# One gap below the large SBUF buffers: every large buffer at a multiple of 512 bytes

## The reference

```python
h = x
for i in range(2):
    if i == 0:
        h = h + retention_branch(rms_norm(h, ret_norm), ret_w_in, ret_w_out)
    else:
        h = h + pool_branch(rms_norm(h, pool_norm), pool_w_in, pool_w_group, pool_scale, pool_w_out)
    gate = sigmoid(rms_norm(h, ple_norm[i]) @ ple_w_gate[i])
    h = h + gate * (p[i] @ ple_w_proj[i])
return rms_norm(h, final_norm)
```

## Time and profile before

| | |
|---|---|
| time, median of 3 runs | 1616.88 us (1616.85 to 1617.04) |
| span of the profiled execution, first to last instruction | 1614.2 us |
| TensorE busy | 1592.1 us, 99% |
| TensorE weight loads busy | 1317.2 us, 82% |
| VectorE busy | 988.7 us, 61% |
| ScalarE busy | 726.6 us, 45% |
| granted TensorE clock, mean | 0.998 |
| from HBM | 296.60 MB, 185 GB/s over the span |

### The profile page before, as it was taken

How to read it: one execution, slowest core, us unless ns; L and a number is a source line. 1 busy time by engine, 2 the same in 40 slices (tenths; PEclk the granted TensorE clock), 3 DMA queues, 4 the chain that set the end, 5 groups by cost and what they waited for, 6 DMA issues and landing times.

```text
span 1614.2 us, 19583 instructions
## 1 busy us (share of the span) xinstructions
PE 1592.1 (99%) x7240; PEld 1317.2 (82%) x7240; DVE 988.7 (61%) x1218; ACT 726.6 (45%) x888; POOL 5.1 (0%) x13
## 2 busy tenths in 40 slices
PE   7999999999999999999999999999999999999997
PEld 6888888888888888888888888888888888888885
DVE  5676666657566666657656565645565565555665
ACT  6444434344444434345645444344434443445543
POOL 0000000000000000000000000000000000000000
PEclk9999999999999999999999999999999999999999
DMA  9545554545545455545455445555554555555451
GB/s 354 177 166 180 186 197 168 195 163 193 182 171 182 182 185 178 194 181 204 160 179 209 183 183 180 185 182 191 184 186 170 206 182 182 198 192 186 179 188 73
DMA packets 42806, 299.24 MB, mean 185 GB/s; under 512 B 4848, under 2 KB 4864, under 8 KB 7312
## 3 DMA queue, kind: packets, MB, share of 16 engines
q1 hardware_dynamic: 41408, 292.60, 50.5%
q0 software_dynamic: 1072, 5.06, 0.8%
q10 hardware_dynamic: 288, 1.05, 0.2%
HBM read 296.60 MB, written 2.10 MB: 185 GB/s over the span
## 4 chain that ended last, share of the span: by engine, by line
PE 98%; DVE 1%; DMA 1%; ACT 0%; issue 0%; SPq 0%; ACTq 0%
PE accB L303 11%; PE accB L304 11%; PE accB L305 11%; PE accC L303 10%; PE accC L304 10%; PE accC L305 10%; PE accA L303 10%; PE accA L305 10%; PE accA L304 10%; PE side L326 2%; DMA h<-in_x_dram 1%; PE side L368 0%; PE side L366 0%; PE side L367 0%; PE side L415 0%; PE side L416 0%
## 5 line engine op out<-in xcount | busy, mean ns | idle before, releaser
L799 DVE TENSOR_TENSOR w_lo<-w_raw,w_hi 128x1024 fp32r<-128x1024 f32 x552 | 669.7, 1223 | 424.4 <-ACT w_hi L566 420.0
L566 ACT CAST w_hi<-w_raw 128x1024 fp32r<-128x1024 f32 x552 | 579.3, 1054 | 628.0 <-PE accB L305 266.7
L303 PE MATMUL accA<-w_hi,xa_hi 128*128 128x512 f32 x512 | 201.2, 393 | 0.9 <-DVE w_lo L799 0.9
L305 PE MATMUL accA<-w_hi,xa_lo 128*128 128x512 f32 x512 | 199.7, 390 | 0.0
L304 PE MATMUL accA<-w_lo,xa_hi 128*128 128x512 f32 x512 | 199.7, 390 | 0.0
L303 PE MATMUL accC<-w_hi,xa_hi 128*128 128x512 f32 x384 | 150.7, 392 | 0.0
L304 PE MATMUL accC<-w_lo,xa_hi 128*128 128x512 f32 x384 | 149.6, 390 | 0.0
L305 PE MATMUL accC<-w_hi,xa_lo 128*128 128x512 f32 x384 | 149.5, 389 | 0.0
L304 PE MATMUL accB<-w_lo,xa_hi 128*128 128x512 f32 x384 | 149.4, 389 | 0.0
L303 PE MATMUL accB<-w_hi,xa_hi 128*128 128x512 f32 x384 | 149.4, 389 | 0.0
L305 PE MATMUL accB<-w_hi,xa_lo 128*128 128x512 f32 x384 | 149.4, 389 | 0.0
(11 more groups left out here) (183 smaller groups left out, 2120.3 us busy)
## 6 DMA issues: line engine op xcount, KB each, us to landing
w_raw<-in_stream_dram SPq DMA_DIRECT2D x275, 1024.0 KB, 4.8
h<-in_x_dram SPq DMA_DIRECT2D x4, 512.0 KB, 9.8
w_raw<-in_stream_dram SPq DMA_DIRECT2D x2, 512.0 KB, 7.2
dec<-in_decay_dram POOLq DMA_DIRECT2D x1, 1024.0 KB, 8.7
fgain<-in_final_gain_dram POOLq DMA_DIRECT2D x1, 1024.0 KB, 5.1
out_dram<-emb ACTq DMA_DIRECT2D x2, 512.0 KB, 3.1
out_dram<-emb SPq DMA_DIRECT2D x2, 512.0 KB, 2.6
bnd_raw<-in_band_dram POOLq DMA_DIRECT2D x1, 768.0 KB, 7.8
```

What stands on the lines that cost most here:

```text
L303: pe.matmul(acc[pair][t][:], xh, wh, start=first and b == 0, stop=False)
L305: mm = pe.matmul(acc[pair][t][:], xl, wh, start=False, stop=last and b == UNIT - 1)
L566: act.copy(w_hi[:, r % RING, :], w_raw[:, r // 2, (r % 2) * 1024:(r % 2 + 1) * 1024]).then_inc(hi_ready, 1)
L799: dve.tensor_tensor(w_lo[:, r % RING, :], w_raw[:, r // 2, (r % 2) * 1024:(r % 2 + 1) * 1024], w_hi[:, r % RING, :].bitcast(F32), ALU.subt ...
```

## The change

The small buffers, and `warm` from the end, are asked for first. Behind them comes one padding buffer of as many bytes as the next multiple of 512 wants, rounded down to 32-byte steps, since each buffer begins at a multiple of 32 anyway: here 32 bytes. `idn` is then at 16512 (remainder 128), `w_raw` at 19968 and the arena at 179712, both at remainder 0, and so is every other large buffer. No instruction is added, removed or moved.

```diff
+        idn = sb("idn", [P, P], F32)
+        gain = sb("gain", [P, STAGES - 1, KD], F32)
+        pscale = sb("pscale", [P, GROUPS * KG], F32)
...
+        junk = sb("junk", [P, TT, COL], mybir.dt.bfloat16)
+        warm = sb("warm", [P, 1], F32)
+        LINE = 512
+        sb("line_pad", [P, (-nc.sbuf_base % LINE) // 32 * 8], F32)
         w_raw = sb("w_raw", [P, RAW, PIECE * COL], F32)
         w_hi = sb("w_hi", [P, RING, UNIT * COL], F32R)
         w_lo = sb("w_lo", [P, RING, UNIT * COL], F32R)
...
         sig = sb("sig", [P, TT, COL], F32)
         p_raw = sig[:].rearrange("p t (k n) -> p t k n", n=SEQ)
-        idn = sb("idn", [P, P], F32)
...
-        junk = sb("junk", [P, TT, COL], mybir.dt.bfloat16)
-
-
         ARENA_KB = 48
         arena0 = nc.sbuf_base
+        assert arena0 % LINE == 0
         sb("arena", [P, ARENA_KB * 256], F32)
-        warm = sb("warm", [P, 1], F32)
```

More of the change, by code:

```diff
@@ L99, in sem @@
             return ctx.enter_context(nc.semaphore(name))
+        idn = sb("idn", [P, P], F32)
+        gain = sb("gain", [P, STAGES - 1, KD], F32)
+        pscale = sb("pscale", [P, GROUPS * KG], F32)
+        ssq = sb("ssq", [P, STAGES, TT, NC], F32)
+        rs = sb("rs", [P, STAGES, TT], F32)
+        stats = sb("stats", [P, TT, 6], F32)
+        mv = sb("mv", [P, TT, 2], F32)
+        rstd = sb("rstd", [P, TT], F32)
+        nx2 = sb("nx2", [P, TT], F32)
+        nt2 = sb("nt2", [P, TT], F32)
+        ni2 = sb("ni2", [P, TT], I32)
+        junk = sb("junk", [P, TT, COL], mybir.dt.bfloat16)
+        warm = sb("warm", [P, 1], F32)
+        LINE = 512
+        sb("line_pad", [P, (-nc.sbuf_base % LINE) // 32 * 8], F32)
         w_raw = sb("w_raw", [P, RAW, PIECE * COL], F32)
```

## The result

The changed kernel takes 1607.13 us (median of 4 runs, 1606.89 to 1607.45) against 1616.87 us for the kernel before on the same chip: a ratio of 0.9941, with a 95% interval of 0.9926 to 0.9955. It is faster by 9.7 us, the interval reaching from 7.3 to 12.0 us. The forecast was 1609.0.

What follows compares the result with a forecast made beforehand. TensorE's matmul count times start-to-start distance was taken as the bound. Arena matmuls 7.7 us plus transitions 0.2 us, all else zero, gave 7.9 us less: 1609.0 us from the 1616.88 median, 8-in-10 range 1602 to 1617.5.

Steps and rivals of the forecast that it cites:

- equal remainders: Main case: matching stationary and streamed remainders in the arena gives 1609.0 us, own range 1607.5 to 1610.5; 65%.
- What bounds the kernel: TensorE, busy 1592.1 of 1614.2 us: time is the number of matmuls times their start-to-start distance.
- Which remainder counts: Whether the remainder against the other operand or against 512 sets the matmul distance; the prediction chose the other operand.
- The arena's matmuls, 7.7 us: 1152 matmuls with `xb` and `dT` go from 233.35 to 226.67 ns each, gaining 7.7 us.
- Transitions, net 0.2 us gained: Disturbances at 0.04 us each: 13 fewer at arena returns and `values`, 9 more behind transposes in `xb` and `dT` stages.
- Transposes, nothing: `idn` stays at 128 while its partners move to 0; no effect, though 6.7 ns on all 320 would be 2 us.
- The other 5472 stationary operands, zero: `xa`, `oT`, `pT` matmuls keep equal remainders, so no change; bounds 73 us down and 37 us up.
- VectorE, ScalarE, transfers: No address effect on both engines; weight landings hidden; only x at the start exposed, +-0.3 us.
- Nothing moves: Rival: the arena's 6.7 ns comes from something else, such as its high place in memory; 1616.9 us, 11%.
- Zero is better than merely equal: Rival: operands off a multiple of 256 or 512 cost extra; 1520.9 us at full price, near 1565 at half; 14%.
- Slower: Rival: at remainders 0 and 0 the stream doesn't settle at 226.7 ns, costing 5472 matmuls 24 to 37 us; 1633 to 1646; 10%.

Runs made afterwards that it cites:

- the kernel at 448: Changed kernel with padding chosen so all large buffers and the arena begin 448 bytes past a multiple of 512; 1608.26 us, ratio 0.9949.
- the kernel with 192 bytes of padding: Kernel before, old buffer order, with only 192 bytes of padding between junk and the arena, putting the arena at remainder 128; 1608.51 us, ratio 0.9954.
- the last experiment: Changed kernel with pscale asked for ahead of idn, so idn too is at a multiple of 256; 1608.78 us, ratio 0.9952.
- the kernel at 128: Changed kernel with padding chosen so all large buffers and the arena begin 128 bytes past a multiple of 512; 1608.36 us, ratio 0.9948.

## Why the prediction was right, and where a term was off

The forecast gain was 7.9 us and the measured one 9.7. The time of 1607.1 us lies in the range for 8 in 10, but just outside the 1607.5 to 1610.5 us that the prediction gave equal remainders by themselves. Between the spans the gain is 8.6 us: the transitions brought 1.0 us more than forecast, the steady distance 0.1 less, the start and the rest 0.2 less. The other 1.1 us is the scatter of the profiled executions against their medians.

**What bounds the kernel.** Right. TensorE's matmuls set the time, nothing else moved, and 1152 matmuls at another distance appear in the end to their full sum.

**Which remainder counts.** Right: the difference. The reading of the earlier trace rows, that 448 beside 448 behaves like 128 beside 128 behind a disturbance, was borne out by the kernel at 448. What no row could tell was the modulus. The prediction worked with remainders modulo 512, and the runs show 256.

**The arena's matmuls, 7.7 us.** The surplus of the long distances fell by 7.5 us: 7.6 of the steady distance went, and 0.1 of disturbances now shows (the prediction had put 0.3 on these).

**Transitions, net 0.2 us gained.** This is the term that was mis-sized; the net gain is 1.2 us. The prediction expected one disturbance less at 13 places and one more at 9. Measured, the disturbances in `xa`, `oT`, `pT` and `values` fell by 1.3 us. It had left out that the other pieces, too, work from the arena (`scores`, the transposes of `qk`, `yn` and `gm`, the window sums) and hand over to products that lay elsewhere. The numbers that follow are long distances up to the next piece, on average. Behind `scores` three became none. Behind `values` four became one, and that one is the matmul right ahead of the next transposes. Behind the transposes of `yn` five became three. Behind `scores` and `values` the kernel with 192 bytes of padding shows the same none and one, so there it is the arena's alignment that does it. Behind the transposes of `yn` it shows seven, so there the gain depends on `idn` or on something else that this kernel doesn't share. Which, the last experiment leaves open. The price of 0.04 us each, too, was that of the longest kind: in the same trace the surplus behind `scores` is 0.02 us, behind most transposes of `qk` and `yn` 0.024, behind `values` 0.01. For the nine matmuls of `values` themselves it held: 0.3 us for 8 calls.

**Transposes, nothing.** Right for the transposes' own time: from start to start they take 109 to 110 ns in both kernels, whether the remainder of `idn` is that of the other operand or not. They had an effect on the matmuls behind them that the prediction didn't price.

**The other 5472 stationary operands, zero.** Right: `xa` runs at 226.7 ns as before. The bounds of 73 us down and 37 us up were bounds of ignorance; the kernel with the streamed buffers moved by 192 shows that the upper one was a real price (1650.8 us), had the change made the difference 64 there.

**VectorE, ScalarE, transfers.** Right: 1226 and 1225 ns for the two products of the earlier trace rows, a landing of 4.7 us for the earlier trace rows's 4.8. The start of the products came 0.6 us earlier, 0.5 of it a shorter wait for x. The wait was 3.9 us again in the kernel at 128 and 3.5 in the one at 448, so it isn't shown that the address of `h` does it.

```profile
L909 DVE TENSOR_TENSOR yn<-yn,sig 128x1024 f32<-128x1024 f32 x8 | 9.8, 1226 | 1.0
...
L922 DVE TENSOR_TENSOR sig<-sig,emb 128x1024 f32<-128x1024 f32 x7 | 8.6, 1225 | 9.9 <-ACT sig L627 9.9
...
w_raw<-in_stream_dram SPq DMA_DIRECT2D x275, 1024.0 KB, 4.7
```

**The rivals.** "Nothing moves" is refuted by the result and by the 192 bytes. "Zero is better than merely equal" is refuted by the kernels at 128 and 448, within their intervals of some 0.15%, and by 226.7 ns in all of them. "Slower" didn't come: the stream settles at 226.7 at remainder 0 as well.

**What stays open.** Why a difference costs anything. The trace shows the weight load for the next matmul starting with each matmul and running under it, and a difference of addresses slows the stream by up to 7.6 ns; a conflict between the two reads would do that, but no run here takes the load away or moves it in time. The Trainium skill ("SBUF — State Buffer", Who interferes with whom) gives PE two read ports, one for the moving operand and one for LDWEIGHTS, and says that PE never waits on anyone; 1650.8 against 1607.1 us for nothing but other addresses of the two operands doesn't agree with that. The 13.3 ns between 226.7 and 213.3, which is half of the 427 ns measured at half the clock, are also unexplained; no placement tried touches them.

## What to carry to other kernels

Where float32 matmuls of 512 columns stand back to back and set the time, let the stationary and the streamed operand have the same address modulo 256 bytes; another difference cost 2.3 to 7.6 ns of 227 here, 2.7% of this kernel with a difference of 64 in all products. No price showed in the 128-column transposes, and other types and shapes weren't tried. Which common remainder it is doesn't matter, and one padding buffer ahead of the region that is off is enough. To find such a region, compare the distance from start to start of the same matmul form with different buffers, since the weight load's own duration doesn't show it.

## What was not expected of the hardware

- The cost has a period of 256 bytes, comes in full with the first 32 bytes (233.3 ns), and isn't symmetric: the stationary operand 64 bytes ahead costs 6.6 ns, 64 behind (192) 2.3 ns, with the stationary buffer moved or the streamed one alike.
- Behind a short piece of other matmuls the steady distance can take up to 10 matmuls to come back, mostly at 229 to 237 ns and in nearly the same sequence each time. How many depends on where that piece's operands lie: behind `scores` five before and none in the changed kernel. Nine matmuls of `values` at a difference of 0 ran at 229 to 232 ns behind products at another remainder.
- The number of matmuls at the start that ran at 427 ns, before the clock of 2.4 GHz was granted, was 1 to 8 in the profiled executions of this study; at 200 ns each that alone can shift a time by over 1 us.
